# Sparse attention's pairs: one power for two pairs, one step more of lag, and the lower half of a sum taken by ScalarE and GpSimd

## The chip, the cores and the metric

The kernel runs on one core of one Trainium2 chip. The metric is the time of one execution on the device, in microseconds (us). A core has engines that each work through a queue of their own, in order: PE (TensorE, the matmuls; PEld is its weight load), DVE (VectorE), ACT (ScalarE), POOL (GpSimd) and SP (SyncE, here only transfers). They wait for each other through semaphores.

## The reference, cut to what matters

The model is two transformer blocks in a row over 512 tokens of width 1024; the second block's mixer is a sparse attention (NSA) with 16 heads in 4 groups of 4, head width 64. Its output per head is a gated sum of three attentions:

```
p_cmp = masked_softmax(einsum('bghtd,bngd->bghtn', qg, k_cmp), ...)
o_cmp = einsum('bghtn,bngd->btghd', p_cmp, v_cmp)
p_sel = masked_softmax(einsum('bghtd,bgtkd->bghtk', qg, k_g), pos <= t)
o_sel = einsum('bghtk,bgtkd->btghd', p_sel, v_g)
p_win = masked_softmax(einsum('bghtd,bkgd->bghtk', qg, k_w), wmask)
o_win = einsum('bghtk,bkgd->btghd', p_win, v_w)
o = g_blk[..., 0:1] * o_cmp + g_blk[..., 1:2] * o_sel + g_blk[..., 2:3] * o_win
return o.reshape(B, QB, G * Hg * dk) @ w_out
```

At 512 tokens the selected blocks and the window both come to plain causal attention, with their own keys and values. The change touches only the part that computes `o_sel` and `o_win` and adds them to `o_cmp`.

## The kernel before

Numbers in full precision are carried as a high part and a low part (`hT`/`hL`, `nprobT`/`nprobL`, `w_high`/`w_low`), each good for a fast matmul, and products are sums of three or two matmuls.

The stage in question, "the pairs", works through 64 pairs in the order of the list `npairs`: key group g (4), token tile t (4 of 128 tokens), head pair hp (2), branch b (2: selected or window). A pair is two heads, two units of 128 query tokens against (t+1)*128 keys, so the width of a pair grows from 128 over 256 and 384 to 512 columns four pairs at a time, and 16 pairs make one group g. Every engine runs a loop over steps s; all work of a unit moves through them like this (line numbers of the profile):

- PE, `scores(p)` at step p-1 (L2668 to L2670): the scores of a pair, six matmuls, into two of four PSUM banks; it waits until the exponentials two pairs back are done.
- DVE at step p (L2759): one reduce for the negated maxima of both units.
- ACT at step p (L2743): two exponentials from PSUM into `nprob` (8 slots), each with its sum read out behind it into `np_total`.
- POOL (L2793): one power, sum to the minus one, of 128x2; then for each of the two units (L2795) a multiplication of the exponentials by that reciprocal and by the gate.
- PE, `turn(p)` at step p+2 (L2680): transposes of the scaled probabilities, unit by unit into two banks that alternate; each waits until the unit before in its bank has been read.
- ACT at step p+3 (L2729): copies of the transposed unit, the high part `nprobT`. DVE at step p+3 (L2766): the low part `nprobL`.
- PE, `values(p)` at step p+4 (L2695, L2696, L2699): the products with the values. The 128 rows of the result are two halves of 64 that belong together: values' high part in the upper, their low part in the lower. Two pairs (both branches) sum into one of two banks; this is an output o = p // 2, 32 in all.
- DVE at even steps from 6 (L2777, L2778): the output's upper half, then the lower half, added to `oT`, where `o_cmp` already stands. The second add waits for the first through a semaphore (`link`). `p_added` counts outputs.

Once a group is complete, its two chunks of `oT` (128x512) are split for the output projection: ACT copies the high part (`chunk_high`, L372, at steps with s % 16 = 6 and 10 of the next group; it waits for `p_added`), POOL subtracts the low part (L2800). The last two chunks are split after the loop, by ACT and DVE. Within a step ACT's queue holds: copies of an earlier pair, the exponentials of this one, a chunk's copy if there is one. PE's holds: values, scores, turns. The order is written out by hand; nothing is planned at run time.

After the stage comes `nsaO`, the output projection. It is bound by PE, takes the chunks one after the other, four token tiles by three matmuls each, and waits for chunks 6 and 7 by themselves. Its weights come through `ring`, are split into `w_high` by ACT (L344) and `w_low` by POOL (L352), three tiles ahead.

Of the kernel before, what the change touches and what calls it, by code (L numbers as in the profile page):

```python
# [23 lines left out]
ALU = mybir.AluOpType  # L24
# [3 lines left out]
P = 128  # L28
# [7 lines left out]
HD = 64  # L36
# [118 lines left out]
class Chain:  # L155


    def __init__(self, eng, sem):
        self.eng, self.sem, self.n = eng, sem, 0

    def __call__(self, ins):
# [5 lines left out]
def build(nc, w, out):  # L167

    ctx = ExitStack()
    with ctx:  # L170
# [2080 lines left out]
        def w1_at(i):  # L2251
# [10 lines left out]
            sem(f"n_{k}", nsa) for k in  # L2262
            ("c_scored", "c_masked", "c_exped", "c_scaled", "c_turned", "c_copied", "c_summed", "c_done", "c_chain", "k_high", "k_low"))
        k_twice = [sem(f"n_k_twice{g}", nsa) for g in range(NSA_G)]

# [236 lines left out]
        def _(v):  # L2502
            link = Chain(v, c_chain)

# [108 lines left out]
        def _(sp):  # L2613
# [21 lines left out]
        n_np = len(npairs)  # L2635
        (p_scored, p_peaked, p_exped, p_inverted, p_scaled, p_turned, p_high, p_low, p_summed, p_added, p_chain, o_high, o_low, o_low_v) = (
            sem(f"np_{k}", nsa) for k in
            ("scored", "peaked", "exped", "inverted", "scaled", "turned", "high", "low", "summed", "added", "chain", "o_high", "o_low", "o_low_v"))
        np_peak = [stat[:, 20 + 2 * i:22 + 2 * i] for i in range(2)]
        np_total = [stat[:, 24 + 2 * i:26 + 2 * i] for i in range(3)]  # L2640
        np_recip = [stat[:, 30 + 2 * i:32 + 2 * i] for i in range(2)]

# [4 lines left out]

        minus_one = stat[:, 36:38]

# [7 lines left out]
        def _(pe):  # L2657
# [58 lines left out]

        def chunks_at(s):

            return [2 * (s // 16) - 2 + (s % 16 - 6) // 4] if s >= 16 and s % 16 in (6, 10) else []

        @block.scalar
        def _(a):
            for s in range(n_np + 3):
                for v_ in ((2 * s - 6, 2 * s - 5) if s >= 3 else ()):
                    t = npairs[v_ // 2][1]
                    a.wait_ge(p_turned, v_ + 1)
                    if v_ >= 4:
                        a.wait_ge(p_summed, v_ // 2 - 1)
                    nc.scalar.activation(nprobT[:, v_ % 4, 0:(t + 1) * P], bank[4 + v_ % 2][:, 0:(t + 1) * P],  # L2729
                                         ACT.Copy).then_inc(p_high, 1)  # L2730
                if s < n_np:
                    wd = (npairs[s][1] + 1) * P
                    a.wait_ge(p_peaked, s + 1)
                    if s == 2:

                        a.wait_ge(k_low_g, NSA_G)
                    for i in range(2):
                        v_ = 2 * s + i
                        if v_ >= 8:
# [3 lines left out]
                        nc.scalar.activation(nprob[:, v_ % 8, 0:wd], bank[2 * (s % 2) + i][:, 0:wd], ACT.Exp,  # L2743
                                             bias=np_peak[s % 2][:, i:i + 1], accum_out=np_total[s % 3][:, i:i + 1]).then_inc(p_exped, 1)
                    for c in chunks_at(s):
                        chunk_high(a, c)
            for c in (6, 7):
# [3 lines left out]
        def _(v):  # L2751
            link = Chain(v, p_chain)
            for s in range(n_np + 6):
# [7 lines left out]
                for v_ in ((2 * s - 6, 2 * s - 5) if 3 <= s < n_np + 3 else ()):  # L2761
# [6 lines left out]
                if s >= 6 and s % 2 == 0:  # L2768

                    o = (s - 6) // 2  # L2770
                    g, t, hp, _ = npairs[2 * o]
# [12 lines left out]
        def _(g_):  # L2784
            nc.gpsimd.memset(minus_one, -1.0).then_inc(zeroed, 1)
            g_.wait_ge(zeroed, 3)
            for v_ in range(2 * n_np):
                g, t, h, kb = unit_of(v_)
                wd = (t + 1) * P
                p, i = v_ // 2, v_ % 2  # L2790
                if i == 0:
                    g_.wait_ge(p_exped, v_ + 2)
                    nc.gpsimd.tensor_tensor(np_recip[p % 2], np_total[p % 3], minus_one, ALU.pow).then_inc(p_inverted, 1)  # L2793
                    g_.wait_ge(p_inverted, p + 1)
                nc.gpsimd.tensor_scalar(nprob[:, v_ % 8, 0:wd], nprob[:, v_ % 8, 0:wd], np_recip[p % 2][:, i:i + 1],  # L2795
                                        gates[:, t, h, 1 + kb // 4:2 + kb // 4], ALU.mult, ALU.mult).then_inc(p_scaled, 1)
                if v_ % 2 == 1:
                    for c in chunks_at(v_ // 2):
                        g_.wait_ge(o_high, c + 1)
                        nc.gpsimd.tensor_tensor(hL[:, place[c], :], oT[:, c, :], hT[:, place[c], :], ALU.subtract).then_inc(o_low, 1)  # L2800

# [39 lines left out]
        def after_pairs_(pe, i):  # L2841
# [5 lines left out]
            else:  # L2847
                pe.wait_ge(p_added, n_np // 2)

        nsa_out, _, norm2 = token_stage(block, "nsaO", (hT, hL), ND, [('nsa_w_out_2', BANK)] * 2, residual_add, all_v,  # L2850
# [22 lines left out]
        def value_parts(c, t, ps, link):  # L2873
# [7 lines left out]

        (q_high, q_low, x_scored, x_peaked, x_exped, x_scaled, x_turned, x_high, x_low, x_summed, o_high_, o_low_, x_chain) = (
            sem(f"x_{k}", cross) for k in
            ("q_high", "q_low", "scored", "peaked", "exped", "scaled", "turned", "high", "low", "summed", "o_high", "o_low", "chain"))
        cq0 = state["used"]
# [111 lines left out]
        def _(v):  # L2997
            link = Chain(v, x_chain)

# [119 lines left out]
```

## Time and profile before

| | us |
|---|---|
| median of 3 runs | 1770.75 (1769.94 to 1770.77) |
| the profiled execution | 1771.35 |
| its span, first to last instruction | 1769.6 |
| PE busy | 1714.8 (97%) |
| DVE busy | 956.7 (54%) |
| ACT busy | 845.3 (48%) |
| POOL busy | 963.8 (54%) |
| the pairs stage, from the first scores to the last values | 1054.9 to 1200.5 |

The spans come from the hardware profiler. A busy time counts the instructions of one engine; matmuls overlap each other, so PE's busy time is not PE at its peak. "Idle before" an instruction is time in which its engine had nothing running, with what ended it. A timeline gives start and duration; "x2" means two equal instructions in a row, merged.

### The profile page before, as it was taken

What the parts mean: (1) busy time and instruction counts of PE and PEld (TensorE: products, weight loads), DVE (VectorE), ACT (ScalarE), POOL (GpSimd) and SP (SyncE); (2) the same over time, 40 slices, a digit from 0 to 9 for tenths busy, and PEclk for the clock granted to TensorE, in tenths of its full rate; (3) what the DMA queues carried; (4) which work ended last, traced back from release to release, by engine and by line L of the source; (5) the groups of instructions that cost most, each with busy time, mean ns of one, the idle gap of its engine ahead of it and who ended that gap; (6) DMA issues with size and microseconds to landing.
All of it is one profiled execution on the core that took longest, in us unless ns stands there. A gap on an engine that the chain in (4) does not pass through costs nothing. (4 is left out here: it accounts for less than half of the span.)

```text
span 1769.6 us, 27618 instructions
## 1 busy us (share of the span) xinstructions
PE 1714.8 (97%) x10430; PEld 1523.5 (86%) x10430; DVE 956.7 (54%) x1628; ACT 845.3 (48%) x1686; POOL 963.8 (54%) x701
## 2 busy tenths in 40 slices
PE   6999999999999999999979999999999999999998
PEld 4898887888888998999868978888988889989996
DVE  2147554454538761575048469994324398528842
ACT  4234454332336551464236348884534566426642
POOL 2353432334444874677336449993752368648852
PEclk9999999999999999999989999999999999999999
DMA  6332221123351433233324321012442223323431
GB/s 223 96 84 54 64 74 51 51 61 101 107 176 55 120 111 104 84 96 126 113 65 136 108 64 57 2 37 71 141 125 69 72 84 96 126 78 96 120 120 48
DMA packets 222900, 162.09 MB, mean 92 GB/s; under 512 B 9768, under 2 KB 197296, under 8 KB 222768
## 3 DMA queue, kind: packets, MB, share of 16 engines
q1 hardware_dynamic: 221712, 159.26, 30.2%
q8 instruction: 84, 1.38, 0.3%
q10 hardware_dynamic: 1056, 1.06, 0.2%
q14 instruction: 48, 0.39, 0.1%
HBM read 156.09 MB, written 2.11 MB: 89 GB/s over the span
## 5 line engine op out<-in xcount | busy, mean ns | idle before, releaser
L352 POOL TENSOR_TENSOR w_low<-ring,w_high 128x1024 fp32r<-128x1024 f32 (+2 forms) x223 | 487.9, 2192 | 587.5 <-ACT w_high L344 587.1
L365 PE MATMUL psum<-hT,w_high 128*128 128x512 f32 (+1 forms) x1104 | 378.9, 343 | 7.3 <-PEq L184 6.1
L344 ACT ACTIVATE w_high<-ring 128x1024 fp32r<-128x1024 f32 (+2 forms) x223 | 212.1, 954 | 355.1 <-PE psum L367 354.9
L367 PE MATMUL psum<-hT,w_low 128*128 128x512 f32 (+1 forms) x1104 | 373.2, 338 | 0.0
L366 PE MATMUL psum<-hL,w_high 128*128 128x512 f32 (+1 forms) x1104 | 373.0, 338 | 0.0
L365 PEld LDWEIGHTS psum<-hT,w_high 128*128 128x128 f32 x1104 | 209.9, 190 | 28.7 <-issue 7.3
L367 PEld LDWEIGHTS psum<-hT,w_low 128*128 128x128 f32 x1104 | 209.5, 190 | 22.8
L366 PEld LDWEIGHTS psum<-hL,w_high 128*128 128x128 f32 x1104 | 210.0, 190 | 19.8
L1819 POOL TENSOR_TENSOR w_low<-ffn_sums,w_high 128x512 fp32r<-128x512 f32 x120 | 169.4, 1426 | 49.7 <-ACT w_high L1814 49.5
L365 PE MATMUL psum<-ffn_th,w_high 128*128 128x256 f32 x640 | 181.6, 284 | 4.7 <-DVE ffn_g L2067 3.1
L1819 POOL TENSOR_TENSOR w_low<-ring,w_high 128x512 fp32r<-128x512 f32 x120 | 155.7, 1300 | 54.7 <-ACT w_high L1814 48.8
L367 PE MATMUL psum<-ffn_th,w_low 128*128 128x256 f32 x640 | 181.1, 283 | 0.0
L366 PE MATMUL psum<-ffn_tl,w_high 128*128 128x256 f32 x640 | 181.1, 283 | 0.0
L781 DVE TENSOR_TENSOR x<-x,psum 128x512 f32<-128x512 f32 x56 | 35.9, 682 | 223.6 <-PE psum L367 223.4
L365 PE MATMUL psum<-w_high,ffn_act 128*128 128x512 f32 x352 | 137.2, 390 | 0.0
L366 PE MATMUL psum<-w_low,ffn_act 128*128 128x512 f32 x352 | 137.0, 389 | 0.0
L367 PE MATMUL psum<-w_high,ffn_act 128*128 128x512 f32 x352 | 136.9, 389 | 0.0
L365 PEld LDWEIGHTS psum<-ffn_th,w_high 128*128 128x128 f32 x640 | 122.3, 191 | 5.5 <-DVE ffn_g L2067 3.5
L366 PEld LDWEIGHTS psum<-ffn_tl,w_high 128*128 128x128 f32 x640 | 122.4, 191 | 0.0
L367 PEld LDWEIGHTS psum<-ffn_th,w_low 128*128 128x128 f32 x640 | 122.4, 191 | 0.0
L1814 ACT ACTIVATE w_high<-ring 128x512 fp32r<-128x512 f32 x120 | 75.1, 629 | 72.0 <-PE psum L367 72.0
L365 PE MATMUL psum<-w_high,hT 128*128 128x256 f32 (+2 forms) x320 | 106.7, 333 | 2.0 <-POOL w_low L352 1.3
(443 smaller groups left out, 3758.7 us busy)
## 6 DMA issues: line engine op xcount, KB each, us to landing
ring<-in_w_in SPq DMA_DIRECT2D x58, 512.0 KB, 3.6
ring<-in_ffn_w_up SPq DMA_DIRECT2D x44, 512.0 KB, 3.8
ring<-in_w_gate SPq DMA_DIRECT2D x22, 512.0 KB, 3.7
ring<-in_w_up SPq DMA_DIRECT2D x22, 512.0 KB, 4.8
ring<-in_w_down SPq DMA_DIRECT2D x20, 512.0 KB, 3.7
ring<-in_ffn_w_down SPq DMA_DIRECT2D x20, 512.0 KB, 3.8
ring<-in_nsa_w_in SPq DMA_DIRECT2D x18, 512.0 KB, 3.6
ring<-in_ca_wkv SPq DMA_DIRECT2D x16, 512.0 KB, 3.6
```

Of the source, the lines that this page charges most:

```text
L344: nc.scalar.activation(tile_view(w_high, n, SPLIT), tile_view(ring, n, RING), ACT.Copy).then_inc(w_hi, 1)
L352: nc.gpsimd.tensor_tensor(tile_view(w_low, n, SPLIT), tile_view(ring, n, RING), tile_view(w_high, n, SPLIT), ALU.subtract).then_inc(w_lo, 1)
L365: nc.tensor.matmul(ps, lhsT=sh, rhs=mh, start=first, stop=False)
L366: nc.tensor.matmul(ps, lhsT=sh, rhs=ml_, start=False, stop=False)
L367: return nc.tensor.matmul(ps, lhsT=sl, rhs=mh, start=False, stop=last)
L781: return nc.vector.tensor_tensor(dst, dst, ps, ALU.add)
L1814: nc.scalar.activation(operand_place(w_high, r, j), self.source(r, name), ACT.Copy).then_inc(u_high, 1)
L1819: nc.gpsimd.tensor_tensor(operand_place(w_low, r, j), self.source(r, name), operand_place(w_high, r, j), ALU.subtract).then_inc(u_low, 1)
```

## The change

- POOL's loop runs over pairs of pairs: it waits for the exponentials of both, takes the power of their four sums in one instruction of 128x4 and then multiplies the four units. `np_total` and `np_recip` are 4 columns wide, two buffers each.
- Turns, copies, low parts and values come one step later in every engine's loop.
- DVE adds only the upper half of an output to `oT`, at odd steps from 7. ACT copies the lower half (64x256) out of PSUM into a new tile `lower` (`p_took`), at the end of the odd steps. POOL adds `lower` to `oT`, four pairs at a time (128x256, `fold`), 16 times in all, behind the multiplications of every second of its rounds; the last two after its loop. `p_folded` counts these.
- `chunk_high` waits for `p_folded` instead of `p_added` and stands at s % 16 = 8 and 12. PE waits for `p_took` beside `p_added`.
- The semaphore of the removed `link` goes, and the stages before and after the pairs share one chain semaphore (`Chain.on`).

```diff
                 if b == 0 and o >= 2:
                     pe.wait_ge(p_added, o - 1)
+                    pe.wait_ge(p_took, o - 1)
...
-            for s in range(n_np + 4):
-                if s >= 4:
-                    values(s - 4)
+            for s in range(n_np + 5):
+                if s >= 5:
+                    values(s - 5)
                 if s + 1 < n_np:
                     scores(s + 1)
-                if 2 <= s < n_np + 2:
-                    turn(s - 2)
+                if 3 <= s < n_np + 3:
+                    turn(s - 3)
 
         def chunk_high(a, c):
-            a.wait_ge(p_added, 8 * (c // 2) + 8)
+            a.wait_ge(p_folded, 4 * (c // 2) + 4)
             copy(False, hT[:, place[c], :], oT[:, c, :]).then_inc(o_high, 1)
 
         def chunks_at(s):
-            return [2 * (s // 16) - 2 + (s % 16 - 6) // 4] if s >= 16 and s % 16 in (6, 10) else []
+            return [2 * (s // 16) - 2 + (s % 16 - 8) // 4] if s >= 16 and s % 16 in (8, 12) else []
...
         def _(a):
-            for s in range(n_np + 3):
-                for v_ in ((2 * s - 6, 2 * s - 5) if s >= 3 else ()):
+            for s in range(n_np + 6):
+                for v_ in ((2 * s - 8, 2 * s - 7) if 4 <= s < n_np + 4 else ()):
...
-                        if i == 0 and s >= 3:
-                            a.wait_ge(p_inverted, s - 2)
+                        if i == 0 and s >= 4:
+                            a.wait_ge(p_inverted, s // 2 - 1)
...
+                if s >= 7 and s % 2:
+                    o = (s - 7) // 2
+                    a.wait_ge(p_summed, 2 * o + 2)
+                    if o >= 4:
+                        a.wait_ge(p_folded, o // 2 - 1)
+                    nc.scalar.activation(lower[rows_of(o), o // 2 % 2, :], sum_of(o)[HD:P, :], ACT.Copy).then_inc(p_took, 1)
+                for c in chunks_at(s) if s < n_np else ():
+                    chunk_high(a, c)
...
-                    link(nc.vector.tensor_tensor(dst, src[0:HD], dst, ALU.add))
-                    nc.vector.tensor_tensor(dst, src[HD:P], dst, ALU.add).then_inc(p_added, 1)
+                    nc.vector.tensor_tensor(dst, src[0:HD], dst, ALU.add).then_inc(p_added, 1)
...
-            for v_ in range(2 * n_np):
-                g, t, h, kb = unit_of(v_)
-                wd = (t + 1) * P
-                p, i = v_ // 2, v_ % 2
-                if i == 0:
-                    g_.wait_ge(p_exped, v_ + 2)
-                    nc.gpsimd.tensor_tensor(np_recip[p % 2], np_total[p % 3], minus_one, ALU.pow).then_inc(p_inverted, 1)
-                    g_.wait_ge(p_inverted, p + 1)
...
+            def fold(m):
+                g, t, _, _ = npairs[4 * m]
+                dst = oT[:, 2 * g:2 * g + 2, q_tile(t)]
+                g_.wait_ge(p_added, 2 * m + 2)
+                g_.wait_ge(p_took, 2 * m + 2)
+                nc.gpsimd.tensor_tensor(dst, dst, lower[:, m % 2, :].rearrange("p (h c) -> p h c", c=P),
+                                        ALU.add).then_inc(p_folded, 1)
+
+            for q in range(n_np // 2):
+                g_.wait_ge(p_exped, 4 * q + 4)
+                nc.gpsimd.tensor_tensor(np_recip[q % 2], np_total[q % 2], minus_one, ALU.pow).then_inc(p_inverted, 1)
+                g_.wait_ge(p_inverted, q + 1)
+                for v_ in range(4 * q, 4 * q + 4):
+                    g, t, h, kb = unit_of(v_)
+                    wd = (t + 1) * P
+                    nc.gpsimd.tensor_scalar(nprob[:, v_ % 8, 0:wd], nprob[:, v_ % 8, 0:wd], np_recip[q % 2][:, v_ % 4:v_ % 4 + 1],
+                                            gates[:, t, h, 1 + kb // 4:2 + kb // 4], ALU.mult, ALU.mult).then_inc(p_scaled, 1)
+                if q >= 5 and q % 2:
+                    fold((q - 5) // 2)
+                for c in chunks_at(2 * q):
+                    g_.wait_ge(o_high, c + 1)
+                    nc.gpsimd.tensor_tensor(hL[:, place[c], :], oT[:, c, :], hT[:, place[c], :], ALU.subtract).then_inc(o_low, 1)
+            for m in range(n_np // 4 - 2, n_np // 4):
+                fold(m)
```

## Rows read from the trace of the kernel before

**Rows 1.** Busy time by engine in the first, third and fourth group (us).

```profile
core 0: us, PE busy (x) PEld busy (x) DVE busy (x) ACT busy (x) POOL busy (x), PEclk, DMA share, GB/s
1058.69:1090.67 31.98, 31.19 (x216) 28.00 (x217) 27.84 (x55) 26.89 (x90) 29.99 (x48) 0.93 0.33 96
1126.76:1161.74 34.98, 33.75 (x258) 30.91 (x257) 32.45 (x65) 29.91 (x99) 32.57 (x52) 1.00 0.14 47
1161.74:1196.75 35.01, 33.15 (x248) 29.71 (x246) 32.18 (x64) 29.46 (x95) 32.59 (x51) 1.00 0.01 1
```

**Rows 2.** The chain of waits from 1055 to 1225 us, shares by line.

```profile
by line: issue 19.4%; DVE nprobL L2766 16.8%; DVE stat L2759 12.6%; PE psum L2680 8.9%; DVE oT L2777 5.0%; PE psum L366 4.8%; PE psum L367 4.8%; PE psum L365 4.8%; PE psum L2696 4.2%; PE psum L2695 3.8%; POOL nprob L2795 2.7%; POOL stat L27
```

**Rows 3.** Timeline of ACT: start, us, engine, line, operation [idle before <-releaser].

```profile
1132.08 0.20 ACT L2743 ACTIVATION_READ_ACCUMULATOR nprob<-psum,stat 128x1 f32 x1
1139.10 0.20 ACT L2743 ACTIVATION_READ_ACCUMULATOR nprob<-psum,stat 128x1 f32 x1
1140.84 0.20 ACT L2743 ACTIVATION_READ_ACCUMULATOR nprob<-psum,stat 128x1 f32 x1
1149.82 0.20 ACT L2743 ACTIVATION_READ_ACCUMULATOR nprob<-psum,stat 128x1 f32 x1
1151.66 0.69 ACT L2743 ACTIVATE nprob<-psum,stat 128x512 f32<-128x512 f32 x1 [0.59 <-DVE stat L2759]
1153.00 0.87 ACT L2729 ACTIVATE nprobT<-psum 128x384 fp32r<-128x384 f32 x2
1153.85 0.69 ACT L2743 ACTIVATE nprob<-psum,stat 128x512 f32<-128x512 f32 x1
1158.06 0.20 ACT L2743 ACTIVATION_READ_ACCUMULATOR nprob<-psum,stat 128x1 f32 x1
1167.06 0.20 ACT L2743 ACTIVATION_READ_ACCUMULATOR nprob<-psum,stat 128x1 f32 x1
```

**Rows 4.** Timeline of DVE, step 44: two adds, then the reduce.

```profile
1149.49 0.42 DVE L2777 TENSOR_TENSOR oT<-psum,oT 64x256 f32<-64x256 f32 x1
1149.94 0.43 DVE L2778 TENSOR_TENSOR oT<-psum,oT 64x256 f32<-64x256 f32 x1
1150.40 1.23 DVE L2759 TENSOR_REDUCE stat<-psum 128x2 f32<-128x1024 f32 x1
```

**Rows 5.** Groups of instructions in the stage, shapes apart: busy us, mean ns.

```profile
L2793 POOL TENSOR_TENSOR stat<-stat 128x2 f32<-128x2 f32 x64 | 45.1, 705 | 3.7 <-ACT nprob L2743 3.0
L2795 POOL TENSOR_SCALAR nprob<-nprob,stat,ngate 128x256 f32<-128x256 f32 x32 | 17.6, 559 | 1.7
L2795 POOL TENSOR_SCALAR nprob<-nprob,stat,ngate 128x512 f32<-128x512 f32 x32 | 24.4, 775 | 1.7
L2729 ACT ACTIVATE nprobT<-psum 128x256 fp32r<-128x256 f32 x32 | 11.0, 391 | 0.7 <-PE psum L2680 0.5
```

**Rows 6.** Groups of POOL's two-input instructions over the whole span, shapes apart.

```profile
L352 POOL TENSOR_TENSOR w_low<-ring,w_high 128x512 fp32r<-128x512 f32 x16 | 20.6, 1290 | 42.6 <-ACT w_high L344 42.6
L352 POOL TENSOR_TENSOR w_low<-ring,w_high 128x256 fp32r<-128x256 f32 x24 | 17.7, 739 | 42.9 <-ACT w_high L344 42.8
```

**Rows 7.** Who waited for whom in the stage: us in total, times, longest us.

```profile
ACT nprobT L2729 <- PE psum L2680: 10.7, 24, 1.0
ACT nprob L2743 <- DVE stat L2759: 10.6, 21, 0.7
PEld psum L2680 <- POOL nprob L2795: 6.2, 19, 1.0
```

**Rows 8.** Timeline of all engines at the stage's end.

```profile
1200.54 0.40 PE L365 MATMUL psum<-w_high,hT 128*128 128x512 f32 x1
1201.23 0.39 PE L365 MATMUL psum<-w_high,hT 128*128 128x512 f32 x1
1201.66 1.15 ACT L372 ACTIVATE hT<-oT 128x512 fp32r<-128x512 f32 x2 [2.93 <-DVE oT L2778]
1207.67 2.73 POOL L352 TENSOR_TENSOR w_low<-ring,w_high 128x1024 fp32r<-128x1024 f32 x1 [10.92 <-ACT w_high L344]
```

More of the change, by code:

```diff
@@ L159, in __init__, with on @@
         self.eng, self.sem, self.n = eng, sem, 0
+    def on(self, eng):
+        self.eng = eng
+        return self
     def __call__(self, ins):
@@ L2263, in build @@
             ("c_scored", "c_masked", "c_exped", "c_scaled", "c_turned", "c_copied", "c_summed", "c_done", "c_chain", "k_high", "k_low"))
+        sparse_chain = Chain(None, c_chain)
         k_twice = [sem(f"n_k_twice{g}", nsa) for g in range(NSA_G)]
@@ L2502, in _ @@
         def _(v):
-            link = Chain(v, c_chain)
+            link = sparse_chain.on(v)
             def blocks_low(i):
@@ L2635, in build @@
         n_np = len(npairs)
-        (p_scored, p_peaked, p_exped, p_inverted, p_scaled, p_turned, p_high, p_low, p_summed, p_added, p_chain, o_high, o_low, o_low_v) = (
+        (p_scored, p_peaked, p_exped, p_inverted, p_scaled, p_turned, p_high, p_low, p_summed, p_added, p_took, p_folded, o_high, o_low, o_low_v) = (
             sem(f"np_{k}", nsa) for k in
-            ("scored", "peaked", "exped", "inverted", "scaled", "turned", "high", "low", "summed", "added", "chain", "o_high", "o_low", "o_low_v"))
+            ("scored", "peaked", "exped", "inverted", "scaled", "turned", "high", "low", "summed", "added", "took", "folded", "o_high", "o_low", "o_low_v"))
         np_peak = [stat[:, 20 + 2 * i:22 + 2 * i] for i in range(2)]
-        np_total = [stat[:, 24 + 2 * i:26 + 2 * i] for i in range(3)]
-        np_recip = [stat[:, 30 + 2 * i:32 + 2 * i] for i in range(2)]
+        np_total = [stat[:, 24 + 4 * i:28 + 4 * i] for i in range(2)]
+        np_recip = [stat[:, 128 + 4 * i:132 + 4 * i] for i in range(2)]
+        lower = nsa_tile("lower", [P, 2, 2 * P], 66560)
         def unit_of(v_):
@@ L2646, in unit_of, with rows_of @@
             return g, t, 4 * g + 2 * hp + v_ % 2, 4 * b + g
-        minus_one = stat[:, 36:38]
+        minus_one = stat[:, 136:140]
+        def rows_of(o):
+            return slice(HD * npairs[2 * o][2], HD * npairs[2 * o][2] + HD)
         def sum_of(o):
@@ L2740, in _ @@
                             a.wait_ge(p_turned, v_ - 7)
-                        if i == 0 and s >= 3:
-                            a.wait_ge(p_inverted, s - 2)
+                        if i == 0 and s >= 4:
+                            a.wait_ge(p_inverted, s // 2 - 1)
                         nc.scalar.activation(nprob[:, v_ % 8, 0:wd], bank[2 * (s % 2) + i][:, 0:wd], ACT.Exp,
-                                             bias=np_peak[s % 2][:, i:i + 1], accum_out=np_total[s % 3][:, i:i + 1]).then_inc(p_exped, 1)
-                    for c in chunks_at(s):
-                        chunk_high(a, c)
+                                             bias=np_peak[s % 2][:, i:i + 1], accum_out=np_total[s // 2 % 2][:, v_ % 4:v_ % 4 + 1]).then_inc(p_exped, 1)
+                if s >= 7 and s % 2:
[6 more added lines that the diff above has]
+                    chunk_high(a, c)
             for c in (6, 7):
@@ L2751, in _ @@
         def _(v):
-            link = Chain(v, p_chain)
-            for s in range(n_np + 6):
+            for s in range(n_np + 7):
                 if s < n_np:
@@ L2760, in _ @@
                                             ALU.max, negate=True).then_inc(p_peaked, 1)
-                for v_ in ((2 * s - 6, 2 * s - 5) if 3 <= s < n_np + 3 else ()):
+                for v_ in ((2 * s - 8, 2 * s - 7) if 4 <= s < n_np + 4 else ()):
                     t = npairs[v_ // 2][1]
@@ L2767, in _ @@
                                             nprobT[:, v_ % 4, 0:(t + 1) * P], ALU.subtract).then_inc(p_low, 1)
-                if s >= 6 and s % 2 == 0:
-                    o = (s - 6) // 2
+                if 7 <= s < n_np + 7 and s % 2:
+                    o = (s - 7) // 2
                     g, t, hp, _ = npairs[2 * o]
@@ L2848, in after_pairs_ @@
                 pe.wait_ge(p_added, n_np // 2)
+                pe.wait_ge(p_took, n_np // 2)
         nsa_out, _, norm2 = token_stage(block, "nsaO", (hT, hL), ND, [('nsa_w_out_2', BANK)] * 2, residual_add, all_v,
@@ L2878, in build @@
                                    tiles=2, banks=((4, 5), (6, 7)), vacant=after_ck)
-        (q_high, q_low, x_scored, x_peaked, x_exped, x_scaled, x_turned, x_high, x_low, x_summed, o_high_, o_low_, x_chain) = (
+        (q_high, q_low, x_scored, x_peaked, x_exped, x_scaled, x_turned, x_high, x_low, x_summed, o_high_, o_low_) = (
             sem(f"x_{k}", cross) for k in
-            ("q_high", "q_low", "scored", "peaked", "exped", "scaled", "turned", "high", "low", "summed", "o_high", "o_low", "chain"))
+            ("q_high", "q_low", "scored", "peaked", "exped", "scaled", "turned", "high", "low", "summed", "o_high", "o_low"))
         cq0 = state["used"]
@@ L2997, in _ @@
         def _(v):
-            link = Chain(v, x_chain)
+            link = sparse_chain.on(v)
             def out_low(h, d):
```

6 lines of the change are left out of this document (removed).

## The prediction

> **What bounds the kernel now.** I began with the shares of the whole run and went at once to the stage that the diff touches, the 64 pairs of sparse attention, 1058 to 1201 us. Taken group by group [rows 1], four engines are nearly full at the same time: a group of 16 pairs takes 35.0 us, in which POOL is busy for 32.6, DVE for 32.4, PE for 33.7 (its busy time counts pipelined matmuls twice over in part) and ACT for 29.9. POOL runs back to back, yet the chain of waits [rows 2] hardly goes through it: DVE's lines lead, with "issue" (the hops from engine to engine) between them. So the stage is a loop through all engines, and which one ends it changes with the width of the pair. To see where, I marked the end of the exponentials of single pairs [rows 3], numbering pairs and steps from 0: pair 35 ends at 1132.28, pair 40 at 1141.04, 44 at 1150.02, 47 at 1158.26, 51 at 1167.26. That cuts one period into 8.76 + 8.98 + 8.24 + 9.00 = 34.98 us. In the widest steps the two adds and the reduce stand in a row on DVE [rows 4]: the add at 1149.49, the second at 1149.94, the reduce at 1150.40, and the exponential waits for that reduce to 1151.66, 0.59 us of idle ACT [rows 3].
>
> **Second add leaves DVE.** 32 adds of 0.43 us with the gap to the next go, 0.46 us each [rows 4], 8 in a group. In steps 45 to 47 nothing but ACT's own work is then late. By [rows 3], a step there is the copies (1153.00 to 1153.85, 0.85) and the two exponentials (1151.66 to 1153.00, 1.34), 2.19 us; three steps are 6.57, the new copy of step 45 adds 0.39 (the 128x256 copy out of PSUM [rows 5]), the chunk copy that moves to step 44 adds 0.58 (two in 1.15 [rows 8]). 7.54 against 8.24: 0.7 us gained. Steps 48 to 51 go at PE's pace with narrow exponentials on ACT: I take 9.00 again. In the nine narrower steps DVE loses four adds (1.84 us) and ACT gains four copies (1.56); ACT waits for PE and DVE for 21.3 us in the stage [rows 7], so a part of its copies falls into waits: I take 0.4 of gain (ends 0 and 1.8). Per group 1.1, in four groups 4.4 us.
>
> **ScalarE's copy of the lower half.** 32 copies of 64x256. The trace has none of that shape from PSUM at these partitions; the 128x256 copy at 0.391 us [rows 5] is the nearest row, with 0.3 to 0.45 as ends. They are in the sums above. The copy waits for the pair's sum, which PE forms before the scores that ACT has already used in this step, so that wait is free. PE's added wait, for the copy two outputs back, is for work done two steps earlier: free.
>
> **One power for two pairs.** 64 powers of 128x2 at 0.705 us [rows 5] become 32 of 128x4. No row shows four columns. The ends are 0.705 (all of it fixed) and 1.41 (double); no row is nearer to either, so I take 1.0. The saving is 0.41 for two pairs, 8 times in a group, 3.3 us of POOL; the four folds (128x256, 0.739 us by [rows 6]) put 3.0 back. POOL is as full as before, hence gives nothing by itself.
> The rows for two-input instructions [rows 6] give 0.551 us for 256 columns and so 0.188 us at no columns at all; the power is 0.5 us above that for two columns. The Trainium skill (GPSIMD Engine Reference, section "Elementwise — side-by-side cycle accounting") says that a GpSimd instruction is a software loop over the elements behind a dispatch that is paid once. By that rule the power would be 0.188 + 2 x 0.517 = 1.22 us, an estimate, and the result 0.6 us later than with my 1.0 (three stalls, below, 0.2 us longer each); if the loop's start is the cost, 0.9 earlier. No run here shows which.
>
> **One step more of lag.** The turns and the values move one step back. PE waited for POOL's scaled pair 19 times, 6.2 us [rows 7]; the power now waits for two pairs' exponentials, so the first pair of the two is ready a step later and the extra step only pays that back. I count 0.3 us for the start. The drain is no longer: after the last exponential POOL has a power and four multiplications of 0.775, 4.1 us, where it now has one power less in front and is itself behind by about as much. The wait for the power's result before its sums are written again is behind the turn that ACT has already waited for.
>
> **The wait that is added.** This decides. The chunk copy on ACT (`chunk_high`) waited for sums that had long been added. Now it waits for the fourth fold of the group. For the even chunk it stands at step 24, 40 and 56 (s % 16 = 8), at the end of ACT's step; the fold that it needs is POOL's last instruction for pairs 22 and 23 (38 and 39, 54 and 55), behind a power that can start only when the exponentials of pair 23 are done. From there POOL takes 0.1 (hop) + 1.0 + 0.1 + 4 x 0.55 (multiplications of 128x256, 0.559 [rows 5]) + 0.74 (fold) + 0.1 (hop) = 4.2 us. ACT gets to the wait after its new copy, 0.39, and one step, 1.74 us (pair 39's end at 1139.30 to pair 40's at 1141.04 [rows 3]): 2.1 us. So ACT stands still for 2.1 us (1.8 with a power of 0.705, 2.5 with 1.41). Behind it in its queue are the next pair's copies out of PSUM and the next exponentials; DVE's low parts, PE's turns and the scores two steps on wait for these, and POOL has nothing to scale meanwhile. ACT is the fullest engine in these steps, so I take the whole stall as lost: 3 x 2.1 = 6.3 us. The odd chunk, four steps later, waits for the same fold and finds it done; the last two chunks are copied after the loop.
>
> **The end of the stage.** The last folds put about 1 us between the last sum and the chunk copies (1201.66 [rows 8]). The output projection begins at 1200.54 with chunk 0; a product takes 0.69 us (1201.23) and there are 24 before chunk 6, so it is wanted at 1217. POOL's next weight (1207.67) had waited 10.92 us and its tile is wanted as late. Cost nothing; without that cover, 1 us.
>
> **Sum.** The profiled execution took 1771.35 us (span 1769.6 and 1.75 around it), 0.6 above the median of 1770.75. 6.3 lost, 4.4 + 0.3 gained: 1.6 more, 1772.95 for it, 1772.3 by the median.
>
> **Rivals.**
> *The stall is absorbed.* ACT has 21.3 us of waits in the stage [rows 7]; if the stall takes the place of those that would follow it, only the relief is left: 4.7 less, 1766.0. Against it: in the steps after the stall ACT has the longest work of all engines. PE's own busy time [rows 1] leaves at most 35.0 - 33.2 = 1.8 us in a group, so 4 x 1.8 = 7.2 less, 1763.5, is the most that can come out. Chance 0.23.
> *ScalarE becomes the engine that sets the pace everywhere.* It has 29.9 us in a group of 35.0 and gets 8 x 0.39 = 3.1, and 2.1 of stall: 35.1, with no idle left for the hops. Then the relief on DVE and POOL is worth nothing and the stalls stay: 1770.75 + 6.3 = 1777.0. It decides from the point where the copies no longer fall into ACT's waits, that is when steps 45 to 47 together take 8.2 us instead of 7.5. For it: 10.6 us of these waits are for DVE, whose work shrinks, so they vanish and hold no copy. Against it: 10.7 are for PE, whose work stays. Chance 0.25.
> The forecast has the other 0.52.
>
> **How the numbers follow.** What a measurement of this kernel can tell from no change is 0.2%, 3.5 us: 1767.2 to 1774.3. The forecast's own range, from the power's ends (-0.9 to +1.2) and the nine steps' (0 to 1.8 instead of 0.4, four times: +1.6 to -5.6, of which I hold half likely), is 1768 to 1775. It gives 0.05 to faster, 0.42 to same and 0.05 to slower; the first rival 0.17 faster and 0.06 same; the second 0.20 slower and 0.05 same. Faster 0.22, same 0.53, slower 0.25. A range with a tenth left out at either side reaches to the rivals' times: 1766 to 1777.
>
> **What would show it.** ACT idle before the chunk copies (L372) of steps 24, 40 and 56, released by POOL's fold, about 2 us each and three in number; none would say that the stall is wrong. The power's mean at four columns. Pair 44 to pair 47 near 7.5 us. ACT's waits for DVE's reduce gone from the wide steps. POOL's idle time after each stalled fold. The prediction is wrong if the period between like marks is under 34 us in the groups with a stall, or over 36.5.

## The result and the profile after

The changed kernel takes 1777.81 us (median of 6 runs, 1775.97 to 1779.11) against 1770.35 for the kernel before (6 runs, 1768.14 to 1771.17): ratio 1.0045, 95% interval 1.0034 to 1.0056. It is slower by 7.5 us, where 1.6 had been predicted, and lies just beyond the end of the range, 1777. The profiled execution took 1776.05 us (span 1774.3).

Both traces were cut at the same places: the stage's first scores, the ends of single pairs' exponentials (as in [rows 3]), and the first product of the output projection. Times in us, differences of two starts or ends in the timelines:

| | before | after | change |
|---|---|---|---|
| first scores to pair 3 | 7.03 | 6.61 | -0.42 |
| pair 3 to 19 | 35.37 | 33.39 | -1.98 |
| pair 19 to 35 | 34.98 | 37.88 | +2.90 |
| pair 35 to 51 | 34.98 | 37.91 | +2.93 |
| pair 51 to 63 | 25.98 | 27.44 | +1.46 |
| pair 63 to the first product ("drain") | 7.30 | 9.85 | +2.55 |
| stage | 145.64 | 153.08 | +7.44 |

The stage holds the whole difference. What lies outside it is the same code but for semaphores, yet its length varied between 1621.2 and 1625.3 us over the profiles of this study (1623.96 in that of before, 1621.22 after; that is why the two profiled executions differ by only 4.7). In seven of the 14 profiles (e1, e8 and the second of the changed kernel among them, not before and after) 1.5 us of this lie in the stretch from 240 to 270 us behind the stage's end: PE's granted clock is 0.94 there in these seven and 1.00 in the others. The stage repeats far better: two profiles of the changed kernel gave 153.08 and 153.32. So small differences below are read from the stage, and whole times stand beside it. The kernel before was profiled once, so its stage of 145.64 has no second reading.

Groups of instructions of the stage after, shapes apart, as in [rows 5] and [rows 6]:

```profile
L2739 ACT ACTIVATE nprobT<-psum 128x256 fp32r<-128x256 f32 x32 | 10.5, 384 | 1.8 <-PE psum L2689 1.6
L2761 ACT ACTIVATE lower<-psum 64x256 f32<-64x256 f32 x32 | 12.2, 380 | 2.4 <-PE psum L2709 1.6
L2809 POOL TENSOR_TENSOR oT<-oT,lower 128x256 f32<-128x256 f32 x16 | 11.7, 733 | 4.2 <-DVE oT L2793 4.2
L2814 POOL TENSOR_TENSOR stat<-stat 128x4 f32<-128x4 f32 x32 | 32.6, 1020 | 16.6 <-ACT nprob L2753 16.3
L2819 POOL TENSOR_SCALAR nprob<-nprob,stat,ngate 128x256 f32<-128x256 f32 x32 | 17.3, 554 | 0.8
```

The new instructions cost what was assumed: the power of four columns 1.02 us (1.0), the copy 0.38 (0.39), the fold 0.73 (0.74). Some of the waits in the stage, as in [rows 7]:

```profile
DVE nprobL L2782 <- ACT nprobT L2739: 21.4, 29, 2.8
POOL stat L2814 <- ACT nprob L2753: 16.3, 15, 2.4
PE psum L2689 <- DVE nprobL L2782: 10.1, 12, 2.3
ACT nprobT L2739 <- PE psum L2689: 9.3, 18, 1.0
ACT hT L376 <- POOL oT L2809: 6.3, 3, 2.1
ACT nprob L2753 <- DVE stat L2775: 2.6, 7, 0.8
PEld psum L2689 <- POOL nprob L2819: 0.8, 2, 0.6
```

ACT's wait for DVE's reduce fell from 10.6 to 2.6. In its place stand the wait at L376, three times and 6.3 us in sum, and waits of DVE, POOL and PE whose longest (2.8, 2.4, 2.3) are its echo, as the next rows show. The timeline of all engines shows one of the three (the second, step 40):

```profile
1138.43 2.16 POOL L2819 TENSOR_SCALAR nprob<-nprob,stat,ngate 128x256 f32<-128x256 f32 x4
1139.02 0.20 ACT L2753 ACTIVATION_READ_ACCUMULATOR nprob<-psum,stat 128x1 f32 x1
...
1140.30 0.22 PE L2679 MATMUL psum<-const_r 128*128 128x128 f32 x1
1140.56 0.72 POOL L2809 TENSOR_TENSOR oT<-oT,lower 128x256 f32<-128x256 f32 x1
1141.31 0.63 ACT L376 ACTIVATE hT<-oT 128x512 fp32r<-128x512 f32 x1 [2.09 <-POOL oT L2809]
1141.85 0.64 ACT L2739 ACTIVATE nprobT<-psum 128x256 fp32r<-128x256 f32 x2
1142.25 0.76 DVE L2782 TENSOR_TENSOR nprobL<-psum,nprobT 128x256 fp32r<-128x256 f32 x2 [2.75 <-ACT nprobT L2739]
1142.82 1.09 PE L2689 MATMUL psum<-const,nprob 128*128 128x128 f32 x4 [2.30 <-DVE nprobL L2782]
1143.69 1.02 POOL L2814 TENSOR_TENSOR stat<-stat 128x4 f32<-128x4 f32 x1 [2.41 <-ACT nprob L2753]
```

Pair 40's exponentials end at 1139.22. The chunk copy is next in ACT's queue and cannot start before POOL has gone through four multiplications and the fold; the copies of the transposed pair, long ready, stand behind it, and then everybody waits in turn. PE is idle from 1140.52 to 1142.82. Its granted clock in that stretch and in that of the third stall, from a table by windows (behind the busy times of the five engines stands PEclk, 1.00 for 2.4 GHz and 0.50 for 1.2):

```profile
1138.00:1140.00 2.00, 2.00 (x16) 1.76 (x16) 1.49 (x3) 1.23 (x5) 1.90 (x4) 1.00 0.01 4
1140.00:1142.00 2.00, 0.52 (x4) 0.32 (x3) 0.00 (x0) 0.69 (x2) 1.28 (x3) 1.00 0.00 0
1142.00:1144.00 2.00, 1.18 (x6) 1.17 (x7) 1.69 (x4) 1.98 (x7) 0.31 (x1) 0.66 0.04 8
1144.00:1146.00 2.00, 2.00 (x9) 2.00 (x8) 1.20 (x3) 1.79 (x7) 1.90 (x3) 0.50 0.00 0
1146.00:1148.00 2.00, 2.00 (x15) 1.87 (x15) 1.67 (x4) 1.34 (x5) 2.00 (x4) 0.98 0.01 4
...
1180.00:1182.00 2.00, 1.28 (x10) 1.18 (x11) 1.79 (x4) 1.95 (x8) 0.41 (x1) 1.00 0.04 8
1182.00:1184.00 2.00, 1.87 (x15) 1.56 (x14) 1.96 (x4) 2.00 (x8) 1.90 (x3) 1.00 0.00 0
```

Behind the second stall PE goes at half clock, 1.2 GHz, until about 1146; behind the third it stays at 2.4. Behind the first, not shown, the clock falls as behind the second (0.53 and 0.62 in the two windows from 1105 to 1109). The segments that hold the stalls (pair 24 to 28, 40 to 44, 56 to 60) took 11.93, 11.97 and 10.90 us.

In the widest steps the add stands alone, and ACT no longer waits for the reduce [rows 3, 4]:

```profile
1150.97 0.22 ACT L2753 ACTIVATION_READ_ACCUMULATOR nprob<-psum,stat 128x1 f32 x1
1151.06 0.65 ACT L376 ACTIVATE hT<-oT 128x512 fp32r<-128x512 f32 x1
1152.32 0.72 ACT L2753 ACTIVATE nprob<-psum,stat 128x512 f32<-128x512 f32 x1
1153.17 0.42 DVE L2793 TENSOR_TENSOR oT<-psum,oT 64x256 f32<-64x256 f32 x1
1153.62 1.23 DVE L2775 TENSOR_REDUCE stat<-psum 128x2 f32<-128x1024 f32 x1
1158.31 0.22 ACT L2753 ACTIVATION_READ_ACCUMULATOR nprob<-psum,stat 128x1 f32 x1
```

Pair 44 to 47: 1151.19 to 1158.53, 7.34 us; the odd chunk's copy at 1151.06 does not wait. At the stage's end, after the last exponentials:

```profile
1195.15 0.23 ACT L2753 ACTIVATION_READ_ACCUMULATOR nprob<-psum,stat 128x1 f32 x1
1195.40 0.38 ACT L2761 ACTIVATE lower<-psum 64x256 f32<-64x256 f32 x1
1197.27 1.23 PE L2689 MATMUL psum<-const,nprob 128*128 128x128 f32 x8 [1.00 <-DVE nprobL L2782]
1199.41 1.23 PE L2689 MATMUL psum<-const,nprob 128*128 128x128 f32 x8
1201.54 1.23 PE L2689 MATMUL psum<-const,nprob 128*128 128x128 f32 x8
1205.23 0.40 PE L369 MATMUL psum<-w_high,hT 128*128 128x512 f32 x1
```

The same stretch in the trace of before; its first product, at 1200.54, is in [rows 8]:

```profile
1193.04 0.20 ACT L2743 ACTIVATION_READ_ACCUMULATOR nprob<-psum,stat 128x1 f32 x1
1194.63 1.23 PE L2680 MATMUL psum<-const,nprob 128*128 128x128 f32 x8
1196.87 1.23 PE L2680 MATMUL psum<-const,nprob 128*128 128x128 f32 x8
```

Three turns after the last exponential instead of two. From the last turn to the first product it is 3.69 us after and 3.67 before; the turns are 2.13 us apart after (2.24 before). The drain is longer by one round of turn, copies and low parts; the first of the three turns also starts later behind the last exponential, by 0.5 us (1.89 against 1.39), where ACT's new copy goes ahead of the copies (1195.40). Without that copy the drain is 9.40 (e4, below).

### The profile page after: what moved, and what is told of

The parts are those of the page before. It is cut to its first block and busy times, and to the rows that moved or that the text cites. A ratio compares the mean times of both kernels' runs of the same rounds, so it can differ in the third digit from the quotient of the medians.

```text
span 1774.3 us, 27647 instructions
## 1 busy us (share of the span) xinstructions
PE 1714.4 (97%) x10430; PEld 1524.8 (86%) x10430; DVE 950.3 (54%) x1596; ACT 855.4 (48%) x1718; POOL 959.2 (54%) x685
```

## The experiments

Each is the changed kernel with the edit shown, unless it says otherwise. Periods are pair 19 to 35, 35 to 51. Ratios are of whole times, to the kernel before on the same chip; stage, periods and drain (us) are from one profile each.

| kernel | ratio to before (95%) | stage | periods | drain |
|---|---|---|---|---|
| before | | 145.64 | 34.98, 34.98 | 7.30 |
| after | 1.0045 (1.0034 to 1.0056) | 153.08 | 37.88, 37.91 | 9.85 |
| after_again | 1.0052 (1.0039 to 1.0064) | 153.32 | 38.03, 36.91 | 9.85 |
| e1, chunks later | 1.0004 (0.9995 to 1.0013) | 144.41 | 34.66, 34.65 | 9.86 |
| e2, fold first | 1.0003 (0.9994 to 1.0011) | 144.45 | 34.68, 34.67 | 9.85 |
| e3, lag undone | 1.0108 (1.0092 to 1.0123) | 161.76 | 39.78, 38.58 | 8.02 |
| e3b, the same with even adds | 1.0069 (1.0054 to 1.0084) | 157.09 | 38.16, 38.22 | 8.04 |
| e4, power and lag only | 1.0022 (1.0013 to 1.0032) | 148.58 | 35.87, 35.86 | 9.40 |
| e5, lower half only | 1.0027 (1.0017 to 1.0037) | 148.08 | 35.63, 36.73 | 7.25 |
| e6, reciprocal on DVE, lag | 1.0005 (0.9995 to 1.0014) | 144.52 | 34.66, 34.67 | 9.85 |
| e7, the same without lag | 0.9996 (0.9987 to 1.0005) | 143.46 | 34.73, 34.72 | 7.17 |
| e8, e7 with chunks on POOL | 0.9984 (0.9975 to 0.9993) | 140.49 | 33.73, 33.74 | 7.18 |
| e9, e7 without the lower half | 0.9962 (0.9948 to 0.9976) | 139.21 | 33.40, 33.39 | 7.17 |
| e10, lag only | 1.0016 (1.0007 to 1.0026) | 148.59 | 35.86, 35.86 | 9.40 |

**The stall.** Two edits take away the wait's cause from either side. e1 places the chunk copies two steps later:

```diff
-            return [2 * (s // 16) - 2 + (s % 16 - 8) // 4] if s >= 16 and s % 16 in (8, 12) else []
+            return [2 * (s // 16) - 2 + (s % 16 - 10) // 4] if s >= 16 and s % 16 in (10, 14) else []
```

> The changed kernel with its chunk copies two steps later (s % 16 = 10 and 14). Stall theory: the fold that the even chunk needs is done when ACT gets there, so the three waits of 2.1 us and PE's half clock behind two of them go (the stalled segments were 2.94, 2.99 and 1.93 us longer than before): 7 to 8 us less than the changed kernel, which is within 2 us of the kernel before. Rival (ScalarE sets the pace everywhere, because of its 32 copies): the wait only moves, and it stays at least 5 us over the kernel before.

e2 leaves the copies where they are and puts POOL's fold ahead of the round's power and multiplications:

```diff
             for q in range(n_np // 2):
+                if q >= 5 and q % 2:
+                    fold((q - 5) // 2)
                 g_.wait_ge(p_exped, 4 * q + 4)
...
-                if q >= 5 and q % 2:
-                    fold((q - 5) // 2)
                 for c in chunks_at(2 * q):
```

> The changed kernel with each fold ahead of the wait for the exponentials and of the power, instead of behind the four multiplications; chunk copies stay at 8 and 12. Stall theory: ACT's wait goes as in the run with later chunks, and POOL's fold now lies in its idle time: 7 to 8 us less than the changed kernel, within 2 us of the kernel before. Rival (ScalarE sets the pace): at least 5 us over the kernel before.

Stages of 144.41 and 144.45: 8.67 and 8.63 us less than after, and 1.2 less than the one profile of before, though the whole times are not told from before's (+0.6 and +0.5 us, interval about -1 to +2.3). In e1's timeline the chunk copy follows the exponentials at once:

```profile
1139.82 0.22 ACT L2753 ACTIVATION_READ_ACCUMULATOR nprob<-psum,stat 128x1 f32 x1
1139.92 0.65 ACT L376 ACTIVATE hT<-oT 128x512 fp32r<-128x512 f32 x1
```

So the stall costs the whole of itself and more: 8.7 us for 6.3 of waiting. Segment by segment against e1 (8.70 each) the stalls cost 3.23, 3.27 and 2.20. The two dear ones are those with the clock's fall. A second profile of the changed kernel, without an edit, was to tell whether that is chance:

> The changed kernel as it is, once more, for PE's clock behind its stalls. In the first profile the granted clock fell to half for some 3 us after two of the three waits and the stalled segments were 2.94 and 2.99 us longer than before, against 1.93 after the third. Theory (the clock is a part of its own): each stalled segment is again either near 1.9 or near 3.0 us longer, the long ones with half clock granted behind the wait, and their number may differ. Rival (the three differ by what the engines do): the same two are long whatever the clock.

There the segments took 12.05, 10.94 and 11.96: this time the second was cheap. Its windows, at the second stall and at the third:

```profile
1144.00:1146.00 2.00, 0.42 (x3) 0.32 (x4) 0.96 (x3) 1.93 (x6) 0.04 (x1) 1.00 0.00 0
1146.00:1148.00 2.00, 1.85 (x14) 1.65 (x14) 1.94 (x5) 1.95 (x8) 1.44 (x2) 1.00 0.04 8
1182.00:1184.00 2.00, 1.50 (x8) 1.40 (x9) 1.94 (x4) 1.95 (x7) 0.63 (x1) 0.66 0.03 8
1184.00:1186.00 2.00, 2.00 (x10) 2.00 (x10) 0.90 (x4) 1.50 (x6) 1.90 (x4) 0.50 0.00 0
```

Six stalls in two profiles: the four with a fall to half clock took 11.93 to 12.05, the two without 10.90 and 10.94. The segments with the fall are 1.0 to 1.15 us longer, and which stall gets it changes from run to run. The three stalls of e3 (below), where the engines do other work, part in the same way: 12.85 and 12.82 with the fall, 11.61 without.

**The lag.** e3 takes the extra step out of PE's, ACT's and DVE's loops again, and keeps the shared power:

```diff
-                if s >= 5:
-                    values(s - 5)
+                if s >= 4:
+                    values(s - 4)
...
-                if 3 <= s < n_np + 3:
-                    turn(s - 3)
+                if 2 <= s < n_np + 2:
+                    turn(s - 2)
```

> The changed kernel with turns, copies, low parts and values back at the step they had before; power for two pairs, ACT's copy, the folds and the stalled chunk copies stay. Theory that the lag costs the drain: the 2.5 us that the time from the last exponential to the output projection grew (7.30 to 9.85) go, the start loses its 0.4; the segments of steps 15 to 24 of each group (0.8 us longer than before) come back as well if they are the lag's: 2 to 4.5 us less than the changed kernel. Rival (the lag is needed, because the power now waits for the second pair): PE waits for POOL's scaled units, 0.5 us or more in each second step, and the kernel is 5 us or more slower than the changed one.

Its stage is 8.7 us longer than that of the changed kernel. That says little of the lag, for the adds were left at odd steps, now a step later than their sums, and the chunk stall was still in. e3b moves the adds and the copy of the lower half to the even steps and takes the chunks of e1:

```diff
-                if 7 <= s < n_np + 7 and s % 2:
-                    o = (s - 7) // 2
+                if 6 <= s < n_np + 6 and s % 2 == 0:
+                    o = (s - 6) // 2
```

> The run with later chunk copies and the lag undone too, this time with DVE's add and ACT's copy of an output back at the even steps from 6. In the first run without the lag they had stayed at the odd steps, and PE waited 4.7 us for the adds. Theory (the power for two pairs needs the lag): PE still waits for POOL's scaled units and for copies out of PSUM, and the stage is 4 us or more longer than with lag and later chunks (144.4). Rival (the first run was slow only by the place of the add): the drain's 2.5 us come back and the stage is shorter than 144.4.

12.7 us more in the stage than e1, and the wait of [rows 7] for POOL's scaled pair, 6.2 us before, has grown to 22.0 (up to 1200 us; this stage ends at 1210):

```profile
PEld psum L2689 <- POOL nprob L2819: 22.0, 54, 1.0
```

With the shared power the lag is needed: e5, below, differs from e3b by the power alone, one for each pair, and its stage is 9.0 us shorter. What the lag costs by itself e4 and e10 tell. e4 keeps power and lag, and gives both adds back to DVE (no copy, no fold; the chunks wait for the adds, as before):

```diff
-            a.wait_ge(p_folded, 4 * (c // 2) + 4)
+            a.wait_ge(p_added, 8 * (c // 2) + 8)
...
-                    nc.vector.tensor_tensor(dst, src[0:HD], dst, ALU.add).then_inc(p_added, 1)
+                    two_adds(nc.vector.tensor_tensor(dst, src[0:HD], dst, ALU.add))
+                    nc.vector.tensor_tensor(dst, src[HD:P], dst, ALU.add).then_inc(p_added, 1)
```

> One part alone: the power for two pairs and the step of lag, with both adds back on DVE, no copy by ACT, no fold, chunk copies that wait for the adds as before (at 8 and 12). Theory: no stall; the lag costs its 2 us in the drain, POOL's 0.41 us saved for two pairs gains nothing because DVE's two adds end the wide steps again: 1 to 3 us over the kernel before. Rival (POOL is what bounds the stage): its 13 us less of powers show, 4 us or more under the kernel before.

e10 is e4 with one power of 128x2 for each pair, as before:

```diff
-                g_.wait_ge(p_exped, 4 * q + 4)
-                nc.gpsimd.tensor_tensor(np_recip[q % 2], np_total[q % 2], minus_one, ALU.pow).then_inc(p_inverted, 1)
...
+                    if v_ % 2 == 0:
+                        g_.wait_ge(p_exped, v_ + 2)
+                        nc.gpsimd.tensor_tensor(np_recip[p % 2], np_total[p % 3], minus_one, ALU.pow).then_inc(p_inverted, 1)
```

> The kernel before with one step more of lag alone: turns, values and adds a step later, a power for each pair as before, both adds on DVE, no fold. The power and the lag together made the stage 2.9 us longer (drain +2.1, start -0.3, groups +1.1). Theory: the lag makes the longer drain and pays nothing without the shared power: the drain is 9.4 us or more, 2.1 over before; POOL is as full as before, so the periods stay at 34.98 us (within 0.3), and the stage is about 147.4 to 148. Rival: the drain comes from the shared power (POOL holds the last four multiplications back together): the drain here stays at 7.3 and the stage at 145.6. A period over 35.5 would say that the lag itself costs in the groups, too.

e4's stage is 148.58, e10's 148.59, with equal segments from pair 8 on (within 0.02). So the shared power has no part in it: the lag, with the adds and the chunk copies that it moves, costs 2.9 us. The drain is 2.1 of that, as the theory had it; but the periods grew, too, by 0.88, which it had not. The first group (pair 3 to 19) went the other way, 33.96 against 35.37, so the four groups together get 1.3 longer. In e10's waits ACT stands for DVE's reduce longer than before (10.6 in [rows 7]):

```profile
ACT nprob L2752 <- DVE stat L2768: 15.3, 26, 1.0
```

The loss is not in the widest steps, which got shorter (pair 44 to 47: 7.79 instead of 8.24), but from pair 35 to 40, 9.80 instead of 8.76, with 0.35 more up to pair 44. From 35 to 40 both adds stand right ahead of a reduce three times, twice before, and ACT waits 1.9 us for DVE's reduces instead of 0.8. Whether it is the adds' place that does it, or another of the moved instructions, was not tried.

**The lower half.** e5 has the lower half on ACT and POOL, but no lag, no shared power, and the chunks of e1:

```diff
-                g_.wait_ge(p_exped, 4 * q + 4)
-                nc.gpsimd.tensor_tensor(np_recip[q % 2], np_total[q % 2], minus_one, ALU.pow).then_inc(p_inverted, 1)
...
+                    if v_ % 2 == 0:
+                        g_.wait_ge(p_exped, v_ + 2)
+                        nc.gpsimd.tensor_tensor(np_recip[p % 2], np_total[p % 3], minus_one, ALU.pow).then_inc(p_inverted, 1)
```

> The other part alone: ACT's copy of the lower half, one add on DVE, the folds on POOL, with the power pair by pair and without the lag; chunk copies at 10 and 14, where they wait for nothing. Theory (POOL is as full as DVE, so the folds need the room that the shared power makes): POOL has 34 + 3 us in a group and paces the stage, 37 a group, 5 us or more over the kernel before. Rival (only DVE's second add paced the stage): 3 us or more under the kernel before.

POOL is full, 35.06 us busy in a period of 36.73 (the last of the five busy times of this row by windows), and the stage is 2.4 longer than before, the whole time 4.5, a little less than expected.

```profile
1130.62:1167.35 36.73, 34.48 (x258) 30.90 (x257) 29.74 (x56) 32.88 (x107) 35.06 (x55) 1.00 0.13 44
```

The folds can only be had with room on POOL. e6 makes more: the reciprocal on DVE for each pair, no power, still with the lag and the chunks of e1:

```diff
-                nc.gpsimd.tensor_tensor(np_recip[q % 2], np_total[q % 2], minus_one, ALU.pow).then_inc(p_inverted, 1)
...
+                    nc.vector.reciprocal(np_recip[(s - 1) % 4], np_sums[(s - 1) % 4]).then_inc(p_inverted, 1)
```

> The run with later chunk copies, and the inverse of the sums taken by DVE's reciprocal, pair by pair, instead of POOL's power; lag kept. DVE gets 64 instructions of about 0.2 us (a 128x2 reciprocal took 0.17 elsewhere in the trace), 3.2 us a group, POOL loses 8 a group. Theory (with the lag POOL's units are in time anyway, and DVE is close to its end in the wide steps): 0 to 3 us more than the run with later chunks. Rival (POOL's share still bounds): 3 us or more less than it.

e7 is e6 with the loops of e3b, that is without the lag:

```diff
-                if s >= 5:
-                    values(s - 5)
+                if s >= 4:
+                    values(s - 4)
```

> As the run before it, but without the lag (add and copy at even steps). Theory (the lag is there for the power's delay): with a unit scaled within 1.5 us of its exponential no engine waits for POOL, the drain is back at 7.3 us and the stage 2 to 4 us shorter than before's 145.6. Rival (ScalarE's copies and DVE's reciprocals fill the loop): 146 us or more.

e6 equals e1 (144.52 and 144.41), though POOL has 8 us less work in each period (24.39 busy, 32.27 in e1) and DVE 1.3 more (30.60, 29.32): once the folds fit, more room on POOL is worth nothing here. e7, against e6, gains 2.68 in the drain, while its groups are 1.6 longer, most of it (1.24) in the last twelve steps: 1.1 net. So with the lower half moved off DVE the lag no longer lengthens the groups, it shortens them, and what it costs is the drain.

**What paces it then.** e8 lets POOL, idle for 30% of e7's period, make the chunks' high part:

```diff
-                for c in chunks_at(s) if s < n_np else ():
-                    chunk_high(a, c)
...
+                    g_.wait_ge(p_folded, 4 * (c // 2) + 4)
+                    nc.gpsimd.tensor_copy(hT[:, place[c], :], oT[:, c, :]).then_inc(o_high, 1)
```

> The run with DVE's reciprocal and no lag, and the six chunk copies inside the loop moved from ACT to POOL (idle for 40 us of that stage); the last two stay. Theory (ACT now paces the stage: it waits least of all): two copies of 0.52 us fewer in each of three groups, 2 to 3 us off the stage of 143.5 and 1766 to 1767 in time, under both kernels. Rival (the loop through all engines paces it): the stage stays within 0.5 us.

The second period of e7, then of e8:

```profile
1128.45:1163.17 34.72, 33.69 (x259) 30.95 (x258) 30.57 (x72) 32.51 (x107) 24.42 (x39) 1.00 0.12 47
1126.39:1160.13 33.74, 33.36 (x259) 30.89 (x258) 30.56 (x72) 31.52 (x105) 25.72 (x41) 1.00 0.13 48
```

ACT is spared 1.0 us in a period (31.52 busy, 32.51 in e7), and the period is 1.0 shorter, all of it between pairs 40 and 51, where the two copies stood. This version beats both kernels: 1767.14 us against 1769.61 on the same chip, 2.5 us less (1.2 to 4.4). Its stage is 12.6 us shorter than that of the changed kernel and 5.2 shorter than the one profile of before; the whole time shows half of these 5.2. e9 takes from e7 the copy and the fold of the lower half, so that this half is missing from its result:

```diff
-                    nc.scalar.activation(lower[rows_of(o), o // 2 % 2, :], sum_of(o)[HD:P, :], ACT.Copy).then_inc(p_took, 1)
...
-                if q >= 5 and q % 2:
-                    fold((q - 5) // 2)
```

> The run with DVE's reciprocal and no lag, without ACT's copies of the lower half and without the folds: the lower half of every output (the values' low part) is left out of the result. Theory (the copies take on ACT what DVE was spared): 8 copies of 0.38 us fewer in a group, the period of 34.7 us falls by 1.5 to 3. Rival (they fall into ACT's waits and cost nothing): the period stays within 0.5 us.

```profile
1125.93:1159.32 33.39, 33.04 (x259) 30.89 (x258) 30.40 (x72) 29.64 (x99) 21.74 (x35) 1.00 0.15 49
```

The period falls by 1.3 us to 33.4, a little less than expected, though ACT is spared 2.9 (29.64 busy). PE is now the fullest, 33.04 busy; that it is what holds the rest was not tried, and e9 spares POOL its folds as well.

## Why the prediction was wrong

The runs put the change together one part after the other, in the stage: before 145.64; with the lag 148.59 (e10); with the shared power 148.58 (e4); with the lower half on ACT and POOL and no stall 144.41 (e1); with the stall 153.08.

| term | predicted | measured |
|---|---|---|
| one step more of lag: start, drain, groups | -0.3 | +2.95 |
| shared power by itself | 0 | 0.0 |
| second add leaves DVE, copy on ACT | -4.4 | -4.2 |
| stall of the chunk copy, three times | +6.3 | +8.7 |
| sum | +1.6 | +7.4 |

How much falls to the lag and how much to the relief depends on the order in which the parts are put together: with the lower half moved the lag costs 1.1 net (e6 against e7), not 2.95. No order is needed for the three parts without the stall, before to e1: the groups get 3.3 us shorter where 4.4 were forecast (a period 0.32, forecast 1.1), the start 0.45, and the drain gets 2.55 longer where no change was forecast.

- **One step more of lag: the step that failed.** "The drain is no longer" was wrong by 2.1 us (2.55 with the lower half in): I followed POOL to the last pair, where the bound is the round from turn to turn through PE, ACT and DVE, 2.13 us for each pair that is left, and the lag leaves one more. And "the extra step only pays that back" left out what a step's shift does to the rest of the loop: with both adds on DVE ACT waits 15.3 us for its reduces instead of 10.6, and the groups get 1.3 us longer. The 0.3 at the start was about right (0.45 in e10).
- **The stall: the mechanism was right, the size short.** This is the second term that failed. Place, number (three) and length (2.1 us predicted, 6.3 in sum measured) agree with the trace. I took the stall's cost to be its length. Behind four of the six stalls of the changed kernel PE ran at half clock for a while; the segments with it are 1.0 to 1.15 us longer, which was not in the sum. Here it is two of three, 2.1 us. The sign of being wrong that the prediction named, a period over 36.5 us, was there: 37.88 and 37.91.
- **The relief agrees in sum, 4.5 us in the groups (e4 to e1; e2, with the chunk copies in e4's place, the same) against 4.4, and in part by luck:** it is counted from groups that the lag had made 1.3 us longer, and it lies elsewhere: 0.44 in pairs 44 to 47 (0.7 forecast) and 0.77 in the rest of a period (0.4). The 7.34 us of that mark, near the 7.54 forecast, is half the lag's doing (7.79 in e10), which takes it back in pairs 35 to 40. The mark agreed and proved less than I had asked of it; only the whole period tells.
- **The shared power** saves POOL what was worked out, and gives no time by itself (e10 to e4, both adds on DVE). For four columns the trace has 1.020 us against 0.705 for two [rows 5]; a line through both gives 0.158 a column on top of 0.39. The Trainium skill (GPSIMD Engine Reference, "Elementwise — side-by-side cycle accounting") pictures a GpSimd instruction as a loop over the elements behind a dispatch for each instruction. The trace agrees with a part that is paid once and a part that grows, but not with the estimate of 1.22 us made by that rule: its part paid once, 0.188, came from rows of other two-input instructions.
- **The first rival,** a stall absorbed, fell: e1 shows that it costs more than itself. **The second,** ScalarE setting the pace, came within 1 us of the time by other terms: its mark (8.2 us in steps 45 to 47) was not met, and the relief was not worth nothing. Its thought was half right: in e7 work on ACT sets the pace of some steps, for e8's two copies count in full from pair 40 to 51; of the 2.9 us that e9 spares ACT in a period 1.3 count. In e1, with the same period and ACT at 32.4 us, it is likely the same, though not tried there.
- **The end of the stage** cost nothing, as predicted: what follows the first product is 569.0 us in both profiles.

## What to carry to other kernels

A wait for the last instruction in another engine's queue, placed ahead of ready work on a full engine, was paid in full here, and more where TensorE's clock fell behind it; two steps' distance, or the producer put first in its round, avoided it. A step of lag is not free: count the rounds that are left after the last input, through all the engines of the loop. And work moved from one nearly full engine to another brought little: without the stall a period went from 34.98 to 34.66 us. So look also for a cheaper engine or instruction (a reciprocal of 0.16 us for a power of 0.7). Here that alone brought nothing; it let the lag go (1.1 us in the stage) and made room on POOL for the chunk copies (3.0 more).

## What the runs showed of the hardware

The instructions of e8's stage that took over, shapes apart:

```profile
L2778 DVE RECIPROCAL stat<-stat 128x2 f32<-128x2 f32 x64 | 10.2, 159 | 1.5 <-ACT nprob L2752 1.0
L2824 POOL CAST hT<-oT 128x512 fp32r<-128x512 f32 x6 | 3.7, 617 | 0.0
```

DVE's reciprocal of two columns takes 0.159 us where POOL's power takes 0.705. POOL's copy of 128x512 takes 0.617 us, less than half of its two-input instruction of that shape (1.290 [rows 6]) and as little as ACT's (0.634 after). An idle stretch of 2.3 us on PE was followed by half clock in four of six cases, and in both profiles of the changed kernel there was a stall without it.
